# Prompt scores of the sparse branches as paired 64-row matmuls in a hybrid decoder step

## The reference

```python
s = einsum('btghd,bngd->bghtn', q, kv_c[:, :, 0]) * NSA_SCALE          # compressed keys
p_cmp = masked_softmax(s, cmp_end <= q_pos)
o_cmp = einsum('bghtn,bngd->btghd', p_cmp, kv_c[:, :, 1])
...
s = einsum('btghd,bgtnpd->bghtnp', q_rot, kv_s[..., 0, :]) * NSA_SCALE # selected keys
...
s = einsum('btghd,bkgd->bghtk', q_rot, win_kv[:, :, 0]) * NSA_SCALE    # window keys
p = masked_softmax(s, (dpos >= 0) & (dpos < WINDOW) & (win_pos >= 0))
o_win = einsum('bghtk,bkgd->btghd', p, win_kv[:, :, 1])
o = g[:, :, 0] * o_cmp + g[:, :, 1] * o_sel + g[:, :, 2] * o_win
```

## Time and profile before

| | us |
|---|---|
| Median of 3 runs | 675.97 |
| Lowest and highest of them | 671.38, 680.39 |
| Span of the profiled execution | 675.0 |
| Stretch with the prompt's sparse branches | 286 to 541 |
| MLA stretch and end | 541 to 675 |

### The profile page before, as it was taken

The page is one execution under the profiler, slowest core; times in us unless marked ns, Lnnn a source line. Parts: engine busy times, 40 slices in busy tenths (PEclk is TensorE's granted clock), DMA queues, the critical chain, the costliest instruction groups (busy, mean ns, idle before and its releaser), DMA issues. The chain is left out here.

```text
span 675.0 us, 10193 instructions
## 1 busy us (share of the span) xinstructions
PE 609.6 (90%) x3482; PEld 375.2 (56%) x3482; DVE 286.9 (43%) x758; ACT 214.3 (32%) x614; POOL 93.7 (14%) x175
## 2 busy tenths in 40 slices
PE   6889998978897999879999899999999898999995
PEld 3554554555566865554446366666566765465642
DVE  0122202263658455653345334445444345255335
ACT  1330102241324221242343243445245345053310
POOL 0114531110100320420010001021003121000000
PEclk9889997989897989959999989999999998999999
DMA  8916563368407512223302105032401701010101
GB/s 307 263 47 144 106 155 51 47 87 118 100 1 236 212 26 74 74 74 110 109 18 70 57 1 188 1 111 79 125 2 62 289 2 40 1 62 1 63 0 62
DMA packets 42381, 60.34 MB, mean 89 GB/s; under 512 B 8986, under 2 KB 34074, under 8 KB 41722
## 3 DMA queue, kind: packets, MB, share of 16 engines
q1 hardware_dynamic: 42330, 59.69, 32.3%
HBM read 55.43 MB, written 8.41 MB: 95 GB/s over the span
## 5 line engine op out<-in xcount | busy, mean ns | idle before, releaser
L828 PE MATMUL psum<-wring,bufA 128*128 128x512 f32 (+2 forms) x384 | 159.2, 570 | 2.0 <-DMA wring<-in_w_in 2.0
L828 PEld LDWEIGHTS psum<-wring,bufA 128*128 128x128 f32 x384 | 74.9, 200 | 72.8 <-issue 67.4
L1392 ACT ACTIVATE wring<-wring,small 128x128 f32<-128x128 f32 (+3 forms) x96 | 53.9, 561 | 160.4 <-DVE small L1675 160.0
L1675 DVE CUSTOM_DVE_ANT_0 wring<-psum,const 128x128 f32<-128x128 f32 (+3 forms) x96 | 46.6, 486 | 86.5 <-PE psum L1050 75.1
L803 PE MATMUL psum<-const,ring 128*128 128x128 f32 (+2 forms) x360 | 52.2, 281 | 24.7 <-ACT mid L590 11.8
L803 PEld LDWEIGHTS psum<-const,ring 128*128 128x128 f32 (+2 forms) x360 | 37.9, 138 | 38.6 <-ACT mid L590 13.7
L1278 PE MATMUL psum<-ring,comp 128*128 128x512 f32 x128 | 56.5, 595 | 1.5 <-issue 1.5
L803 PE MATMUL psum<-const,wring 128*128 128x128 f32 x272 | 49.6, 280 | 6.8 <-ACT wring L1471 3.9
L803 PEld LDWEIGHTS psum<-const,wring 128*128 128x128 f32 x272 | 34.2, 143 | 33.6 <-issue 18.5
L1050 PE MATMUL psum<-mid,qrT 128*128 128x128 f32 (+3 forms) x128 | 50.1, 475 | 2.2 <-DVE small L1669 2.2
L1081 PE MATMUL psum<-kv,wring 128*128 128x64 f32 x320 | 43.8, 268 | 1.0 <-DVE rtmp L1703 0.8
(11 more groups left out here) (227 smaller groups left out, 811.3 us busy)
## 6 DMA issues: line engine op xcount, KB each, us to landing
wring<-in_w_in SPq DMA_DIRECT2D x4, 2048.0 KB, 8.6
ring<-in_cache_cmp_kv SPq DMA_DIRECT2D x64, 128.0 KB
ring<-in_cache_mla SPq DMA_DIRECT2D x64, 80.0 KB, 1.9
ring<-in_cache_sel_kv SPq DMA_DIRECT2D x40, 128.0 KB, 2.1
ring<-in_state_win_kv SPq DMA_DIRECT2D x8, 512.0 KB, 5.4
ring<-in_w_o SPq DMA_DIRECT2D x1, 4096.0 KB, 13.7
out_s_win<-in_state_win_kv SPq DMA_DIRECT2D x1, 4064.0 KB
wring<-in_cache_sel_kv SPq DMA_DIRECT2D x24, 128.0 KB, 2.1
```

What stands on the lines that cost most here:

```text
L828: ins = pe.matmul(bank[:, 0:w], xT[:, c, t * P:(t + 1) * P], wr[:, b % 2, c, 0:w], start=(c == 0), stop=(c == KC - 1))
L1392: ins = act.activation(Pp[:, n % 4, 0:w], Pp[:, n % 4, 0:w], ACT.Exp, bias=nmp[:, k, h:h + 1], scale=-1.0, accum_out=lp[:, k, h:h + 1])
L1675: ins = dve.tensor_tensor_reduce(Pp[:, n % 4, 0:w], bank[:, 0:w], mask, -(MLA_SCALE if kind == "pmla" else NSA_SCALE), CLAMP, ALU.add, ALU ...
```

## The change

Selected and window scores use only the 64 partitions of their own group, straight out of the transposed keys `selKT` and `winKT`. Heads are taken in the order 0, 4, 1, 5, 2, 6, 3, 7, so that two neighbouring units use different halves of the partitions. Two slots are merged into one entry of the weave, with both scores first. `padK` and GpSimd's `pad` steps go, `PTp` takes their place in `mid`, there are eight `Pp` buffers, and the lags are 4 and 6. MLA units keep their order and single slots, at the new lags.

```diff
+HEADS = [g * HG + hh for hh in range(HG) for g in range(G)]
+UNITS = ([(i, kind, h) for i in range(PT) for kind in KINDS[:3] for h in (range(G) if kind == "pcmp" else HEADS)]
...
-T_LAG, V_LAG = 3, 5
+T_LAG, V_LAG = 4, 6
+PBUF = 8
...
-    cmp += [([("pad", 0)], .5), ([("pad", 1)], .5)]
...
-    p = [(slot(m), cost(m)) for m in range(N_NSA)]
+    def pair(m):
+
+        a, b = slot(m), slot(m + 1)
+        return a[:1] + b[:1] + a[1:] + b[1:]
+
+    p = [(pair(m), cost(m) + cost(m + 1)) for m in range(0, N_NSA, 2)]
     for t in range(PT):
-        p.insert(N_NSA // 2 + 18 + 4 * t, ([("vup", t)], .6))
-    p.insert(N_NSA, ([("qup", 0)], 1))
+        p.insert(N_NSA // 4 + 9 + 3 * t, ([("vup", t)], .6))
+    p.insert(N_NSA // 2 + PT, ([("qup", 0)], 1))
...
-        Pp = take(2048).rearrange("p (s n) -> p s n", s=4)
-        PTp = take(2048).rearrange("p (s n) -> p s n", s=4)
+        Pp = take(PBUF * 512).rearrange("p (s n) -> p s n", s=PBUF)
...
-        padK = take(2 * G * SEQ).rearrange("p (b g n) -> p b g n", b=2, g=G)
+        PTp = take(2048).rearrange("p (s n) -> p s n", s=4)
...
                     if h == 0 and i == 0:
-                        pe.wait_ge(pad_ready, 1 + int(kind == "pwin"))
+                        wait_copied(pe, T, T.at("post", B_WINGATE, NT - 1))
                     g, hh = h // HG, h % HG
-
-                    ins = pe.matmul(bank[:, 0:keys], qrT3[:, hh, q], padK[:, int(kind == "pwin"), g, 0:keys],
-                                    start=True, stop=True)
+                    s, kT = slice(g * HD, (g + 1) * HD), selKT if kind == "psel" else winKT
+                    ins = pe.matmul(bank[:, 0:keys], qrT3[s, hh, q], kT[s, 0:keys], start=True, stop=True)
```

More of the change, by code:

```diff
@@ L145 @@
 KINDS = ("pcmp", "psel", "pwin", "pmla")
-UNITS = ([(i, kind, h) for i in range(PT) for kind in KINDS[:3] for h in range(G if kind == "pcmp" else H)]
+HEADS = [g * HG + hh for hh in range(HG) for g in range(G)]
+UNITS = ([(i, kind, h) for i in range(PT) for kind in KINDS[:3] for h in (range(G) if kind == "pcmp" else HEADS)]
          + [(i, "pmla", h) for i in range(PT) for h in range(H)])
@@ L1059, in turn_p @@
                 for j in range(1 if kind == "pcmp" else i + 1):
-                    ins = turn(bank[:, j * P:(j + 1) * P], Pp[:, n % 4, j * P:(j + 1) * P])
+                    ins = turn(bank[:, j * P:(j + 1) * P], Pp[:, n % PBUF, j * P:(j + 1) * P])
                 ins.then_inc(T.full[u % T.n], 1)
@@ L1387, in exp_unit @@
                         c, s = h * HG + hh, slice(hh * CHP, (hh + 1) * CHP)
[L1388 removed]
+                        ins = act.activation(Pp[:, n % PBUF, s], Pp[:, n % PBUF, s], ACT.Exp, bias=nmp[:, k, c:c + 1],
                                              scale=-1.0, accum_out=lp[:, k, c:c + 1])
@@ L1391, in exp_unit @@
                     w = (i + 1) * P
-                    ins = act.activation(Pp[:, n % 4, 0:w], Pp[:, n % 4, 0:w], ACT.Exp, bias=nmp[:, k, h:h + 1],
+                    ins = act.activation(Pp[:, n % PBUF, 0:w], Pp[:, n % PBUF, 0:w], ACT.Exp, bias=nmp[:, k, h:h + 1],
                                          scale=-1.0, accum_out=lp[:, k, h:h + 1])
@@ L1668, in min_unit @@
                         c = h * HG + hh
-                        ins = dve.tensor_tensor_reduce(Pp[:, n % 4, s], bank[:, s],
+                        ins = dve.tensor_tensor_reduce(Pp[:, n % PBUF, s], bank[:, s],
                                                        C("cmpmask")[:, i * CHP:(i + 1) * CHP], -NSA_SCALE, CLAMP,
@@ L1674, in min_unit @@
                     mask = const[:, a_tri - i * P:a_tri + P]
-                    ins = dve.tensor_tensor_reduce(Pp[:, n % 4, 0:w], bank[:, 0:w], mask,
+                    ins = dve.tensor_tensor_reduce(Pp[:, n % PBUF, 0:w], bank[:, 0:w], mask,
                                                    -(MLA_SCALE if kind == "pmla" else NSA_SCALE), CLAMP,
@@ L1906, in _ @@
                     silu(*step[1:])
[L1907 to L1913, removed]
-                        s = slice(g * HD, (g + 1) * HD)
-                        ins = pool.tensor_copy(padK[s, j, g, :], (selKT, winKT)[j][s, 0:SEQ])
-                    ins.then_inc(pad_ready, 1)
-                    pool.wait_ge(pad_ready, j + 1)
                 if step[0] != "proj" or step[1] in (B_ZMLA, B_ZNSA):
```

1 line of the change is left out of this document (removed).

## The result

The changed kernel takes 703.71 us (median of 4 runs, 698.16 to 707.40); the kernel before, beside it, 678.18. The ratio is 1.042 (95%: 1.037 to 1.047): slower. The forecast was 668 with a range of 658 to 677, so it missed on the wrong side.

The account below looks back on a forecast made before the run. PE's own work was taken as the bound (busy 90% of the span). 675.0 - 14.6 + 7.5 - 2.8 + 1.5 - 1.5 + 2 = 667.1 us; with the runs' median 0.97 above the span, 668 us, range 658 to 677.

Parts of the forecast that it names:

- last condition: From 304 to 541 us: prediction is wrong if the granted clock falls with half-array work; no size or chance given.
- Part 1: Selected and window scores: 32 pairs of 64-row matmuls stream side by side, saving 14.6 us (13.4 to 17.2).
- the lag: Within a score pair: the second head starts behind the first, taken as 0.08 us, 2.6 us over 32 pairs.
- Rivals 1 and 2: Score pairs: streams take turns, 681 us, chance 8%; or passes keep program order, gain 8.6, 673 us, chance 11%.
- Rival 5: Score pairs: the second score waits for its bank until the first is done; no chance of its own.
- Part 2: Entering and leaving 64-row shape around pairs: 0.19 and 0.16 us each, net +7.5 us (+5.9 to +10.5).
- Part 3: Compressed units: three more pairs take 1.55 us instead of 2 x 1.07, saving 2.8 us (2.0 to 3.5).
- Part 4: Order, lag and buffers: +1.5 us of waits in the sparse stretch (-3 to +6.6), -1.5 in MLA.
- rival 3: Early pairs: waits for the transposes' copy double (+6.6 us) and the clock falls for a while; 675 us, chance 11%.
- Rival 4: Sparse and MLA stretches: full overlap, least shape cost, waits -3 and MLA -3; 656 to 663 us, chance 16%.
- the MLA term: MLA stretch: the longer lag covers waits such as 2.05 us at ScalarE's table reload; -1.5 us (0 to -3).

Follow-up runs that it names:

- hybrid2: Changed kernel with padded 128-row single scores at one and two key tiles, 64-row pairs at three and four, lags 3 and 5, six `Pp` buffers: 684.36 us, ratio 1.013.
- hybrid2_qup: hybrid2 with its query-up step two pairs earlier in the weave: 680.20 us, ratio 1.010 to the kernel before.
- rows128_single: Changed kernel with unpadded 128-row scores in single slots, lags 4 and 6 kept: 691.90 us, ratio 1.023 to the kernel before.
- rows64_single: Changed kernel with its 64-row scores in single slots instead of pairs, lags 4 and 6 kept: 717.98 us, ratio 1.057 to the kernel before.
- rows128_paired: Changed kernel with unpadded 128-row scores, its paired order, lags and buffers kept: 693.06 us, ratio 1.024 to the kernel before.
- lag35_qup: Changed kernel with the old lags 3 and 5 and its query-up step two pairs earlier: 697.58 us, ratio 1.038 to the kernel before.

## Why the prediction was wrong

**The step that failed** is its last condition: it named a fall of the granted clock under half-array work as what would make it wrong, called it something that no row could rule out, and gave it neither a term in the sum nor a chance. In the profiles B grows by 30.6 us, more than the whole loss: 26.9 in the four stages of the sparse branches, which is the stretch that the condition named, 9.7 in MLA, which it did not name, and 6.0 less ahead of them. Its comfort, the decode steps of 32 columns that run at 0.97 or more, was read from a stretch that holds full-height scores and values among them.

By cause, as far as the runs show: half-height scores cost about 20 us of clock at lags of 4 and 6 and at 3 and 5 (hybrid2 and hybrid2_qup at 29 to 32 against 49.8 and 49.5, where the order of the first two stages changes too), chiefly in the stage of one tile. There the 64-row scores come in place of 128-row ones among decode steps of a few rows or columns; the second head is late in three of eight pairs, and the pairs are short (0.80 us each, at 1.2 GHz, in a stage of 67). That this is why that stage loses most is not shown. The longer lags cost 6 to 8 us more of B in MLA (2.9 to 9.3 in rows128_single, 4.4 to 12.6 with 64 rows). The two don't add: lags of 3 and 6 alone bring the 128-row kernel to 42.

**Part 1, the overlap** was right for a pair (0.97 us measured, 0.95 forecast) and the lag smaller than taken (0.01 against 0.08 us). Rivals 1 and 2, streams in turn and program order, fall. The Trainium skill's 4 ns for a further tile ("TensorE: Matmul & The Clock Gate", "Measured speedup vs the span model") is near the 0.01 us seen; its rule of strict order (same page, "What overlaps and what doesn't") does not hold for the passes, as the prediction had it, since both heads' first passes start ahead of either second one. **Rival 5**, second scores that wait for their bank, was given no chance and was true, in part or wholly, for 12 pairs of 32. Its reason looked at waits of single scores on VectorE's minimum; up-projections and decode steps also take the two score banks, and a pair needs both free at once. By the prediction's own prices the other 20 save 5 x 0.22 + 5 x 0.43 + 7 x 0.65 + 3 x 0.86 = 10.4 us: the term of 14.6 was some 4 us too large.

**Part 2, shape changes**: read as in the earlier trace rows, the entries take 0.19 to 0.20 us and the exits 0.15, as forecast (0.19 and 0.16). What they cost the kernel may be less: with 64 entries and exits rows64_single has 3.8 us more of A than rows128_single, where 64 x 0.35 less the 4.9 of before would be 17.5. **Part 3**: the compressed pair takes 1.55 us, as forecast, at full clock.

**Part 4** forecast +1.5 for the order: rows128_paired against rows128_single gives A +1.7. PE's waits for the copy of the transposes (now L1473), 6.6 us in 12 times, are 9.4 in 13 from 280 to 544.7 us: between the forecast and rival 3 (12 or more). That wait is a matter of the lags: it is 8.9 us in 13 times in rows128_single too, where no units are paired, and 1.7 in pairs with 3 and 6; so the cover that the prediction found for lags of 4 and 6 was not there. Rival 4, easing waits, is seen in two places: the weight loads' waits for the exponential (2.7 us) are gone, and so is PE's wait of 2.05 us behind the table load. But the MLA term, -1.5 from the longer lag, had the wrong sign: in MLA the waits on ScalarE's copy are 4.9 us in all (3.8 before), scores wait 4.9 us for VectorE's minimum (1.8 before), A rises by 3.4 and B by 9.7: 13.1 us. The moved query step was not followed past GpSimd's rotation: +3.4 in the profile, 3.2 of A by lag35_qup.

**The stage of four tiles**, where most of the profit was to be made, shows why A fell by 3 and not by 8: it went from 71.6 to 76.6 us, with PE busy 68.58 us against 68.61. Five of its eight pairs ran in turn, wholly or in part, and the wait of 3.4 us on GpSimd came on top. With lags of 3 and 6 and the earlier query step its A is 70.0 (78.6 us at 0.89).

Open stays why the lag of the values moves the clock in the stage of one tile and in MLA. The runs show that it does, with A unchanged; which pause or order of pauses tips it they don't show, and moving the output steps did not help. Open is also why the same program holds its low clock for different times (58.7 and 67.2 us for one stage).

## What to carry to other kernels

Before narrowing a matmul, ask what the granted clock will do with it: two half-height matmuls side by side kept the clock up in a block of their own, one half-height matmul at a time did not, though PE was busy throughout. Split a measured time into span times clock and the rest, for every run: here that told a gain of work (-3) from a loss of clock (+31), which stage times alone mix. And when work is paired, try the lags again (here 4 and 6 took 9 us more of A than 3 and 6), check that each pool of banks can hold both halves at once beside its other users, and follow every step that the pairing moves to the queue it waits on.

## What the runs showed of the hardware

- A block of 40 scores of 64 rows and 512 columns, PE busy 68.60 of 68.6 us, was granted 0.50 throughout; the same with 128 rows 0.95, as 64-row pairs in both halves 0.93. At 128 columns: 0.50 against 0.92.
- Two fp32 matmuls in the two row halves, into different banks, start 0.01 us apart and take 0.97 us for 512 columns, when the second bank is free.
- One unit more of lag to the values, with the same instructions, moved the clock's share by 14 us (B 28.1 to 42.3) and the work by less than 1 us (A 646.8 to 645.9).
